# A decoder layer on eight cores: one branch of the merge for half of the tokens moved under two other stages, and PSUM banks of the recurrence split by use

## What is computed

```python
h = rms_norm(x, norm)
proj = h @ w_in                                   # q/k/v, gates, latents, merge gates
hm = mlstm_chunkwise(mq, mk, mv, ig, lf)          # branch A: recurrence over chunks
hm = rms_norm(hm, mh_norm) * sigmoid(m_o) * silu(m_z)
ha = causal_block_attention(qa, ka, v_a) * silu(a_z)                # branch B
hc = memory_attention(c_q, mem_k, mem_v) * silu(c_z)                # branch C
merged = g_m * (hm @ w_br_m) + g_a * (ha @ w_br_a) + g_c * (hc @ w_br_c)
x = x + merged @ w_out                            # g_* = sigmoid(h @ their columns of w_in)
return rms_norm(x, final_norm)
```

## Times and profile before

| | us |
|---|---|
| median of 3 runs (2875.67 to 3246.26) | 2877.27 |
| the profiled execution, span of its slowest core (1) | 2881.3 |
| the quickest core (7) of that execution | 2853.5 |
| PE busy on core 1 | 2739.6 (95%) |
| DVE busy, ACT busy, POOL busy | 1105.2, 813.3, 498.9 |
| 1228 to 1566: recurrence beside dense work | 338 |
| 1566 to 1682: cross attention beside dense work | 116 |
| 1682 to 2649: merge alone | 967 |

### The profile page before, as it was taken

One profiled execution on the slowest core, in us unless ns is written; L12 is line 12 of the kernel. 1 busy time (PEld: TensorE's weight loads), 2 busy tenths in 40 slices (PEclk: granted clock), 3 DMA queues, 4 the chain that ended last, 5 costly groups with the idle time before them and its releaser, 6 DMA issues.

```text
span 2881.3 us, 42326 instructions; the slowest of 8 cores (2853.5 to 2881.3 us)
## 1 busy us (share of the span) xinstructions
PE 2739.6 (95%) x14317; PEld 1363.0 (47%) x14317; DVE 1105.2 (38%) x2091; ACT 813.3 (28%) x1672; POOL 498.9 (17%) x605
## 2 busy tenths in 40 slices
PE   4898999999999999989889899999999999999998
PEld 2443444575546644444444444444444444444443
DVE  3565547447576457445543321111111111111333
ACT  4632135324343334244443311111111111110211
POOL 0000300000110110234332022222222222221000
PEclk8999999999999999999999999999999999999999
DMA  7715653444444433346543654444475655456562
GB/s 194 195 30 132 176 122 70 115 104 106 88 101 111 102 86 69 73 118 142 142 120 106 152 124 77 76 76 76 76 159 82 106 77 77 77 77 116 194 203 87
DMA packets 144387, 317.97 MB, mean 110 GB/s; under 512 B 14896, under 2 KB 73200, under 8 KB 136752
## 3 DMA queue, kind: packets, MB, share of 16 engines
q0 software_dynamic: 42192, 134.79, 29.2%
q1 hardware_dynamic: 99104, 169.99, 18.8%
q10 hardware_dynamic: 2880, 10.49, 1.1%
HBM read 378.29 MB, written 71.70 MB: 156 GB/s over the span
## 4 chain that ended last, share of the span: by engine, by line
PE 87%; DMA 5%; DVE 3%; ACT 3%; issue 2%; SPq 0%; DVEq 0%; ACTq 0%; POOL 0%; POOLq 0%
PE bk L288 86%; DMA mv_109_13609<-MV 1%; DMA xt_14_61<-x 1%; DMA xt_14_61<-mem 1%; DMA cq_140_17857<-CQT 1%; DVE xb_15_62 L308 0%; DMA xt_13_60<-x 0%; DMA QNT<-ob_39_1819 0%; PE bk L490 0%; DMA HCT<-ho_157_17948 0%; SPq L132 0%; DVE Cf_13626 L308 0%; DMA KRT<-ob_38_1818 0%; DMA mb_113_13613<-BH 0%; ACT hm_102_13602 L296 0%
## 5 line engine op out<-in xcount | busy, mean ns | idle before, releaser
L288 PE MATMUL bk<-w_11_53,hT_9_51 128*128 128x512 bf16 (+1 forms) x1152 | 212.3, 333 | 6.6 <-ACT hr_130_13630 L296 2.2
L288 PE MATMUL bk<-w_11_53,hT_8_50 128*128 128x512 bf16 (+1 forms) x1152 | 208.5, 333 | 4.3 <-DVE GIF_49 L301 1.8
L288 PE MATMUL bk<-hT_8_50,w_10_52 128*128 128x512 bf16 x800 | 191.7, 386 | 2.7 <-ACT e_2_57_3175 L296 1.4
L288 PE MATMUL bk<-hT_9_51,w_10_52 128*128 128x512 bf16 x800 | 187.3, 382 | 0.0
L288 PEld LDWEIGHTS bk<-w_11_53,hT_8_50 128*128 128x128 bf16 x1152 | 111.6, 98 | 84.5 <-issue 6.7
L288 PEld LDWEIGHTS bk<-w_11_53,hT_9_51 128*128 128x128 bf16 x1152 | 111.4, 98 | 84.2 <-issue 9.4
L288 PEld LDWEIGHTS bk<-hT_8_50,w_10_52 128*128 128x128 bf16 x800 | 78.6, 100 | 90.4 <-issue 9.1
L288 PEld LDWEIGHTS bk<-hT_9_51,w_10_52 128*128 128x128 bf16 x800 | 78.3, 99 | 85.1 <-issue 1.6
L308 DVE SCALAR_TENSOR_TENSOR tm_176_19254<-sh_181_19381,bk 128x512 f32<-128x512 f32 x31 | 21.3, 687 | 248.0 <-PE bk L288 248.0
L308 DVE SCALAR_TENSOR_TENSOR tm_176_19254<-sh_183_19383,bk 128x512 f32<-128x512 f32 x31 | 21.3, 687 | 247.5 <-PE bk L288 247.5
L288 PE MATMUL bk<-hT_8_50,wg_135_17736 128*128 128x512 bf16 x512 | 115.8, 383 | 0.0
(11 more groups left out here) (509 smaller groups left out, 4796.6 us busy)
## 6 DMA issues: line engine op xcount, KB each, us to landing
wg_135_17736<-wGB POOLq DMA_DIRECT2D x32, 512.0 KB, 5.5
wg_136_17737<-wGB POOLq DMA_DIRECT2D x32, 512.0 KB, 5.1
wg_137_17738<-wGB POOLq DMA_DIRECT2D x32, 512.0 KB, 5.2
w_10_52<-wA POOLq DMA_DIRECT2D x27, 516.0 KB, 11.9
w_11_53<-wA POOLq DMA_DIRECT2D x21, 516.0 KB, 12.4
xt_12_59<-x SPq DMA_DIRECT2D x6, 1024.0 KB, 5.2
wb_170_18593<-wGB POOLq DMA_DIRECT2D x24, 256.0 KB, 3.9
wb_171_18594<-wGB POOLq DMA_DIRECT2D x24, 256.0 KB, 3.9
```

The costliest lines, as they stand in the source:

```text
L288: fw.op("pe", lambda e: e.matmul(bk[o] if not isinstance(o, bass.AP) else o, lhsT=lhsT, rhs=rhs, start=start, stop=stop), reads=reads, wri ...
```

## The change

1. `d1_gen`, new, runs between `mid_gen` and `d_gen`: gate and branch product of causal attention (b = 1) for th = 0, all 16 c, with dense banks 0 and 1. Each result (128 x 512 float32) goes by an SP DMA to the scratch tensor `AP`. It has its own `wb` ring of 2, `pa` tiles of 2, and loads `hb1` (2 MB) at its start by SP.
2. `d_gen` leaves these 16 units out for th = 0, and `aload` brings the scratch back into `acc` (now 4 tiles), two c ahead. Its first three gate weights are loaded at its own start.
3. The ratios of recurrence and cross attention go from 0.34 and 0.7 to 0.24 and 0.5.
4. `misc`, `bub` and `bob` get two banks each: 6 and 7, 4 and 5, 2 and 3.
5. `mb` has 2 tiles instead of 3; the weaving loop gets a `break`, which alters nothing up to the start of the recurrence: the order on each engine is the same until there.

```diff
+    AP_d = dscr("AP", [16, 2, 128, 512], F32)
...
-            misc = bub = bob = Ring(SB)
+            misc, bub, bob = Ring(SB[4:6]), Ring(SB[2:4]), Ring(SB[0:2])
...
-            B2s = tiles("mb", 3, [128, 4, 128], F32, top=True)
+            B2s = tiles("mb", 2, [128, 4, 128], F32, top=True)
...
+        def d1_gen():
+            mem.release(wst["last"], *P["e16"].items, *P["e32"].items)
+            wg, wb = P["wg"], tiles("wb", 2, [128, 8, 128], BF16)
+            h1 = P["hb1"] = mem.alloc("hb1", [128, 8, 1024], BF16)
+            sgs, ps = Ring(tiles("sa", 2, [128, 512], F32)), Ring(tiles("pa", 2, [128, 512], F32))
...
+            bload(0)
+            bload(1)
+            for j in range(4):
+                c = slice(j * 2048, (j + 1) * 2048)
+                fw.dma("sp", h1[:].rearrange("p a b -> p (a b)")[:, c], HAT_d[0].rearrange("p a b -> p (a b)")[:, c], reads=[dr("HAT", 0)], writes=[h1.r] if j == 0 else [], accs=[h1.r] if j else [])
+            for c in range(16):
+                w, w2, sg2 = wg[c % 3], wb[c % 2], []
+                for tb in range(2):
+                    bk, r_bk = DB.next()
+                    for kc in range(16):
+                        mm(bk, r_bk, (slice(None), slice(None)), w[:, kc, :], hcol(kc, tb), kc == 0, kc == 15, [w.r] + rhg(tb))
+                        if kc % 8 == 7:
+                            yield 8 * MM
+                    sg = sgs.next()
+                    act(sg[:], bk[:], AF.Tanh, [r_bk], [sg.r], scale=0.5)
+                    sg2.append(sg)
+                gload(c + 3)
+                for tb in range(2):
+                    bk, r_bk = DB.next()
+                    for kc in range(8):
+                        mm(bk, r_bk, (slice(None), slice(None)), w2[:, kc, :], h1[:, kc, tb * 512:(tb + 1) * 512], kc == 0, kc == 7, [w2.r, h1.r])
+                    t = ps.next()
+                    stt(t[:], sg2[tb][:], 1.0, bk[:], ALU.add, ALU.mult, [sg2[tb].r, r_bk], [t.r])
+                    fw.dma("sp", AP_d[c, tb], t[:], reads=[t.r], accs=[dr("AP", c, tb)])
+                    yield 8 * MM
+                bload(c + 2)
...
-            units = [(th, c, b) for th in range(2) for c in range(16) for b in range(3)]
+            units = [(0, c, b) for c in range(16) for b in (0, 2)] + [(1, c, b) for c in range(16) for b in range(3)]
...
-            ld = {"g": 3, "b": 0}
+            ld = {"g": 0, "b": 0, "a": 0}
...
+            for _ in range(3):
+                gload()
...
             hload(0, 0)
-            hload(0, 1)
+            hload(1, 1)
...
-        sides = [(mla_gen, "MLA0", 0.38), (mlstm_gen, "ML", 0.34), (c_gen, "CZ0", 0.7)]
+        sides = [(mla_gen, "MLA0", 0.38), (mlstm_gen, "ML", 0.24), (c_gen, "CZ0", 0.5)]
```

More of the change, by code:

```diff
@@ L1185, in mlstm_gen @@
             loads(0)
-            for c in range(3):
+            for c in range(2):
                 loads_b(c)
@@ L1333, in c_gen, with gload, bload @@
             mem.release(kmT, vm, *cqs, *czs.items, *Ps.items, *rds.items, *hcs, *hos.items)
+        def d1_gen():
[3 more added lines that the diff above has]
+            sgs, ps = Ring(tiles("sa", 2, [128, 512], F32)), Ring(tiles("pa", 2, [128, 512], F32))
+            def gload(c):
+                if c < 16:
+                    fw.dma("pool", wg[c % 3][:].rearrange("p a b -> p (a b)"), wGB_d[c, 1, :, 0:16, :].rearrange("p a b -> p (a b)"), writes=[wg[c % 3].r])
+            def bload(c):
+                if c < 16:
+                    fw.dma("pool", wb[c % 2][:].rearrange("p a b -> p (a b)"), wGB_d[c, 1, :, 16:24, :].rearrange("p a b -> p (a b)"), writes=[wb[c % 2].r])
+            bload(0)
[24 more added lines that the diff above has]
+                bload(c + 2)
+            mem.release(*wb, *sgs.items, *ps.items)
@@ L1336, in d_gen @@
         def d_gen():
-            mem.release(wst["last"], *P["e16"].items, *P["e32"].items)
             LA = 4
-            units = [(th, c, b) for th in range(2) for c in range(16) for b in range(3)]
+            units = [(0, c, b) for c in range(16) for b in (0, 2)] + [(1, c, b) for c in range(16) for b in range(3)]
             wg = P["wg"]
+            wb = tiles("wb", 4, [128, 8, 128], BF16)
             sgs = tiles("sg", 2 * LA, [128, 512], F32)
-            ld = {"g": 3, "b": 0}
+            ld = {"g": 0, "b": 0, "a": 0}
@@ L1361, in bload, with aload @@
                 fw.dma("pool", t[:].rearrange("p a b -> p (a b)"), wGB_d[c, b, :, 16:24, :].rearrange("p a b -> p (a b)"), writes=[t.r])
+            def aload():
+                c = ld["a"]
+                if c < 16:
+                    ld["a"] += 1
+                    for tb in range(2):
+                        fw.dma("sp", acc[2 * (c % 2) + tb][:], AP_d[c, tb], reads=[dr("AP", c, tb)], writes=[acc[2 * (c % 2) + tb].r])
             def hload(th, b):
@@ L1392, in d_gen @@
             yield ("need", "HM1")
-            hb = [mem.alloc("hb0", [128, 4, 8, 256], BF16), mem.alloc("hb1", [128, 8, 1024], BF16), P["hb2"]]
+            hb = [mem.alloc("hb0", [128, 4, 8, 256], BF16), P["hb1"], P["hb2"]]
             hload(0, 0)
-            hload(0, 1)
+            hload(1, 1)
             for u in range(LA):
@@ L1403, in d_gen @@
             tmps = Ring(tiles("tm", 2, [128, 512], F32))
-            acc = tiles("acc", 2, [128, 512], F32)
+            acc = tiles("acc", 4, [128, 512], F32)
             merged = [mem.alloc("mer0", [128, 16, 1024], BF16), None]
             wo, gfin = [None] * 4, None
+            aload()
+            aload()
             def wo_load(n4, t):
@@ L1436, in d_gen @@
                         mm(bk, r_bk, (slice(None), slice(None)), w[:, kc, :], (hb[0][:, 2 * tb:2 * tb + 2, kc, :] if b == 0 else hb[1][:, kc, cols] if b == 1 else hb[2][:, 4 * tb:4 * tb + 4, kc, :]), kc == 0, kc == 7, [w.r, hb[b].r])
-                    sg, a = sg2[tb], acc[tb]
-                    if b == 0:
+                    sg, a = sg2[tb], acc[2 * (c % 2) + tb]
+                    if b == 0 and th == 1:
                         stt(a[:], sg[:], 1.0, bk[:], ALU.add, ALU.mult, [sg.r, r_bk], [a.r])
@@ L1448, in d_gen @@
                 bload()
+                if th == 0 and b == 2:
+                    aload()
                 if th == 0 and c == 15:
@@ L1513, in dense_all @@
             yield from mid_gen()
+            yield from d1_gen()
             yield from d_gen()
-        sides = [(mla_gen, "MLA0", 0.38), (mlstm_gen, "ML", 0.34), (c_gen, "CZ0", 0.7)]
+        sides = [(mla_gen, "MLA0", 0.38), (mlstm_gen, "ML", 0.24), (c_gen, "CZ0", 0.5)]
         st = {"gen": None, "i": 0, "d": 0.0, "s": 0.0, "ratio": 1.0, "need": None}
@@ L1551, in build @@
                     st["d"] = st["s"] / st["ratio"]
+                    break
             if st["gen"] is None:
```

11 lines of the change are left out of this document (5 added, 6 removed).

## The result

The changed kernel takes 2930.56 us (median of 4 runs, the lowest 2927.87); the kernel before 2878.55 in its runs beside it. The ratio is 1.018, 95% interval 1.016 to 1.020. The prediction was 2875, with a range that ended at 2902. In some executions the cores of one die run at a lower clock and need longer; ratios leave out those where this is plain. So the change costs 52 us where no change was forecast, and lies outside the range on the slow side.

A forecast was written before the change was run, and what follows sets the result against it. It took PE's idle time and slow clock in the recurrence and cross attention as the room, some 70 us. From 2881.3, 55 removed and 55.5 added, less 4, gave 2877.8, shaded to 2875 us; range 2838 to 2902.

The forecast's parts named there:

- (a) to (c): Recurrence and cross attention: PE's idle waits removed, 20.8 us for shared banks, 12 for loads, 5 for `ho` and dense evacuations.
- (f): Recurrence: head 3's state update waits for DVE's accumulate of head 2, behind the normaliser; 34 us added, bounds 27 and 59.
- (g): Recurrence, heads 0 and 1 with nothing dense between: head 1 waits for head 0's accumulate; 6 us added.
- (e): Recurrence and cross attention: slow-clock matmuls behind removed waits regain speed; 12 us given back.
- (h): Recurrence: new waits at head 3 bring slow-clock matmuls behind them; 6 us added, bounds 0 and 22.
- (d): Recurrence and cross attention: each removed wait saves PE some 0.16 us beyond its idle time; 5 us for about 30.
- rival C: Slower: head 3's waits reach 3 us in at least 10 chunks, each bringing the slow clock; 2897 us, chance 0.17.
- (i): Start of `d1_gen`: PE waits for the late load of `hb1`; 4 us added, and 1 for the clock.
- (j): Start of `d_gen`: PE waits for the first gate weight `wg`, asked for late; 2 to 3 us added.
- (k): Causal attention's branch product on two banks beside cross attention waits for DVE's reads; 2 us added, bounds 0 and 8.
- rival D: Clearly slower: with two `pa` tiles DVE waits for a scratch store in each of 16 units; 2931 us, chance 0.05.
- B: Gain of half the room: the normaliser starts sooner, head 3 finds its banks free or nearly; 2841 us, chance 0.26.

## Why the prediction was wrong, point by point

- **(a) to (c), removed, 37.8 forecast.** Right in kind and a little low: 46.4 of idle time went (53.9 on core 1 before; of all but `Cf`, `hb` and `wg`, 7.5 remain on core 5). The cause was half wrong: one ring with the smaller ratio had only 13 left of the ring waits' 25.
- **(f), 34 forecast, the step that failed first.** Measured at head 3 are 45.0 in 14 chunks, and 4.5 in the first chunk. I took the normaliser's start from one chunk, 2.4 after the outputs, and called the chunk at 6.0 an exception that the smaller ratio would thin out. Neither holds. Over 14 chunks before it was 2.08 to 6.02, mean 3.4; after, with the smaller ratio, again 3.4. In these chunks it is set by whether a dense evacuation stands just ahead of the normaliser in DVE's order, and when that bank's matmuls end. From the line of before alone: the normaliser's 3.6 and the accumulate's end 0.6 later make a wait of start + 3.6 + 0.6 - 4.5, 3.1 on average (4.5 is when head 3 would come; the 4.1 of the prediction was early), with 0.33 for the second matmul 3.4 a chunk: 48 in 14 chunks. In three of them head 3 comes 1.7 later, which takes 5 off: 43, against 45.0 measured. The whole of (f), 49.5, lies inside my bounds of 27 and 59; I had put the point by the one clean chunk.
- **(g), 6 forecast.** 58.7 - 49.5 = 9 measured; inside its bounds. (58.7 is all idle time of core 5 that `Cf` ended; the view leaves out pieces under 0.15 and shows 58.4.)
- **(e) and (h), the clock, with (d): a second failed step, as large in the sum.** I counted 5 + 12 given back and 6 + 1 added. On the timelines I added up by how much dense matmuls followed each other in more than 0.216 us without waiting: 5 to 12 on the cores before, 18 to 21 after, 10 to 17 with one ring (six cores of each; two lack some records). So nothing was given back and some 9 to 11 were added; the granted clock in the recurrence of core 5 is 0.95, where I had said 0.97 to 0.99. The stages less PE's waits say the same: 1359 to 1367 before, 1373 to 1376 after, 1359 to 1368 with one ring. What (d) gave back doesn't show apart from this. On core 5 after, eight of the nine waits of 3.08 and over up to 1674 were followed by 1.3 to 2.0 of such loss, and two (2.19 and 1.83, with 1.3 and 1.9) of the ten between 1.1 and 2.4. The point at 3.0 that rival C named was about right, but I had waits of 2.2 there, and they were 3 to 4.8 in seven chunks. The Trainium skill, TensorE: Matmul & The Clock Gate, section "A second HAM failure mode: psum-queue depth-cycling", tells of this pattern; the trace agrees in direction, with some 10 us, not the 22 of my upper bound.
- **(i), 4 + 1 forecast.** 9.7 on core 5, 6.7 to 10.2 on the others. There are two parts. The issue was late: `d1_gen`'s first gate starts at 1615.76, and SP's queue had been held for 7.4 us by the load of `mg`, which waits until POOL has multiplied by the tile that it overwrites, behind the normaliser. The row of SP's waits:

```profile
SPq L71 <- POOL hmt L302: 7.4, 1, 7.4
```

and its timeline, `hb` being the four loads of `hb1`:

```profile
1618.85 0.32 SPq L132 DMA_DIRECT2D mg<-MG  x1
1619.26 0.38 SPq L132 DMA_DIRECT2D CZ<-e  x1
1619.73 2.61 SPq L132 DMA_DIRECT2D hb<-HAT  x4
```

  So `hb1` was asked for 4.0 after the gate's start, where I had it at once. And it landed late: the last of the four was issued at 1621.12 and PE went on at 1634.12, 13.0 later, for 8.6 in the earlier trace rows.
- **(j), 2.5 forecast.** 12.7 in two waits, 5.2 to 12.7 by core. The DMA issues of core 5 at the start of `d1_gen` (columns as in the earlier trace rows):

```profile
wb<-wGB POOLq DMA_DIRECT2D x2, 256.0 KB, 11.3
wg<-wGB POOLq DMA_DIRECT2D x1, 512.0 KB, 13.4
```

and at the start of `d_gen`, 1845 to 1870:

```profile
hb<-HMT ACTq DMA_DIRECT2D x4, 512.0 KB, 9.9
wg<-wGB POOLq DMA_DIRECT2D x4, 512.0 KB, 15.0
wb<-wGB POOLq DMA_DIRECT2D x4, 256.0 KB, 22.1
acc<-AP SPq DMA_DIRECT2D x4, 256.0 KB, 15.0
AP<-pa SPq DMA_DIRECT2D x2, 256.0 KB, 12.1
```

  Where the first three `wg` landed after 5.3, 7.7 and 10.1 before (the first two in the earlier trace rows), they took 9.9, 13.3 and 16.7 here, and the first was the first wait: 18 DMAs of 256 or 512 KB stand in these 25 us, the four of `acc`, the last two stores to `AP` and the first three `wg`, which the change puts there, among them. The fourth `wg`, issued at 1866.1, took 18.5 and was the second wait, for which the prediction had nothing.
- **(k), (l), rival D.** (k) measured 1.4 at most (`sa`). DVE waits for no store to `AP` on any core: the time that D gave (2931) was met by chance, its cause was not there.
- **The rivals.** B needed a normaliser that starts sooner: it didn't. C was right in kind, (f) longer and the clock lost behind it, but stopped at 2897, since it allowed only 3 us for head 3's wait. As measured the sum is -46.4 + 58.7 + 9.7 + 12.7 = 34.7 of idle time (53.9 to 88.7) and 9 of clock, 44 of the 45.5 between the two slowest cores, where my sum had 0.5. Of the 43 between, 19 are (f) and (g), 19 the clock with (d), 16 the idle time of (i) and (j), less 9 that (a) to (c) gave more and 2 of (k). With (f) read from all chunks, 46 for 34 in 15 chunks, my sum would have been 2890; with (h) at its upper bound besides, 2906, outside my range too.

## What to carry over

When a ring of banks gets shorter, find for each use the instruction that frees the bank and everything that stands ahead of it in its engine's order, and read its lateness in every repetition of the loop, not in the one that looks clean: here the late chunks made the mean. The wait that came from the order on another engine was removed by distance (a ring that two uses share in turn) and for the larger part by order, while two banks showed no cost for the uses whose readers were not behind the normaliser. A load's time to landing is not to be taken from another place alone: at the joints it was 9.9 to 18.5 where the rows had 5.3 to 8.6.

## What the runs showed of the chip

- Waits of PE have a tail: on core 5, behind eight of nine waits of 3.08 us or more the next dense matmuls ran slow and lost 1.3 to 2.0 us more; behind waits of 1.1 to 2.4 in the same stage two of ten did.
- The first three 512 KB loads of `wg` landed 5.3, 7.7 and 10.1 us after their issue before, and 9.9, 13.3 and 16.7 at the start of `d_gen` in the change, with 17 other DMAs in the same 25 us; the fourth took 18.5.
- A removed wait for a load came back at other loads and banks: with `hb` and `wg` gone, `cq` grew from 6.0 to 11.8 as a mean of the cores, and the time stayed. By which resource they are tied is not shown.
